# High and low parts of a weight unit stored in pairs in one tile, instead of in two tiles

## The reference

```python
# first block, per layer (D_MODEL 1024, D_FF 2816)
h = _rmsnorm(x, g_pre_ffn[l])
gate, up = jnp.split(h @ w_ffn_in[l], 2, axis=-1)
f = (jax.nn.silu(gate) * up) @ w_ffn_out[l]
x = x + _rmsnorm(f, g_post_ffn[l])
# second block, per layer
x = x + 0.5 * swiglu(rms_norm(x, ffn1_norm[l]), ffn1_w1[l], ffn1_w2[l])
x = x + hybrid_mixer(rms_norm(x, mix_norm[l]), ...)
x = x + 0.5 * swiglu(rms_norm(x, ffn2_norm[l]), ffn2_w1[l], ffn2_w2[l])
```

## Time and profile before

| what | value |
|---|---|
| two timed runs | 3475.27 and 3480.95 us, median 3478.11 us |
| the profiled execution | 3470.74 us, its span 3468.9 us |
| granted TensorE clock, mean | 0.994 |
| TensorE busy (matmuls) | 3365.4 us, 97% of the span |
| weight loads busy | 2884.7 us, 83% |
| VectorE busy | 2462.7 us, 71% |
| ScalarE busy | 1617.0 us, 47% |
| GpSimd busy | 55.9 us, 2% |
| moved by DMA | 318.95 MB, mean 92 GB/s |

### The profile page before, as it was taken

How to read it: one execution, slowest core, us unless ns; L and a number is a source line. 1 busy time by engine, 2 the same in 40 slices (tenths; PEclk the granted TensorE clock), 3 DMA queues, 4 the chain that set the end, 5 groups by cost and what they waited for, 6 DMA issues and landing times.

```text
span 3468.9 us, 49474 instructions
## 1 busy us (share of the span) xinstructions
PE 3365.4 (97%) x19557; PEld 2884.7 (83%) x19557; DVE 2462.7 (71%) x3512; ACT 1617.0 (47%) x2387; POOL 55.9 (2%) x84
## 2 busy tenths in 40 slices
PE   7999999999999999999999999999999989999999
PEld 5678988767998799887687899889988767788997
DVE  8669854759882888557895698559864888658863
ACT  4645543455562466326524356425542562335642
POOL 1000000000000000000000000000000000000000
PEclk9999999999999999999999999999999999999999
DMA  4123323212332233232133233323333213322332
GB/s 141 50 73 98 99 97 109 82 49 82 102 114 99 76 113 110 95 104 60 49 91 91 97 98 110 100 94 98 110 104 97 75 44 90 92 97 86 110 104 85
DMA packets 339642, 318.95 MB, mean 92 GB/s; under 512 B 31768, under 2 KB 312164, under 8 KB 339428
## 3 DMA queue, kind: packets, MB, share of 16 engines
q1 hardware_dynamic: 335588, 307.95, 28.0%
q0 software_dynamic: 2048, 6.16, 0.5%
q10 hardware_dynamic: 1792, 1.88, 0.2%
HBM read 313.84 MB, written 2.10 MB: 91 GB/s over the span
## 4 chain that ended last, share of the span: by engine, by line
PE 80%; DVE 15%; ACT 3%; issue 2%; DMA 0%; POOL 0%; DVEq 0%; POOLq 0%
PE products L797 31%; PE products L938 24%; PE products L836 7%; PE small L836 6%; PE small L938 4%; PE products L1199 2%; DVE w_lo L2152 2%; DVE seven_x L2404 1%; PE products L1396 1%; DVE conv L2939 1%; DVE X L2172 1%; DVE x_sums L2393 1%; ACT w_hi L1522 1%; PE small L1273 1%; DVE mla_prob L2599 1%
## 5 line engine op out<-in xcount | busy, mean ns | idle before, releaser
L2152 DVE TENSOR_TENSOR w_lo<-raw,w_hi 128x2048 fp32r<-128x2048 f32 x190 | 435.1, 2290 | 482.7 <-ACT w_hi L1522 482.4
L1522 ACT ACTIVATE w_hi<-raw 128x2048 fp32r<-128x2048 f32 x190 | 363.8, 1915 | 833.1 <-PE products L797 579.8
L797 PE MATMUL products<-a_hi,w_hi 128*128 128x512 f32 (+1 forms) x1216 | 490.8, 404 | 12.8 <-DVE a_lo L2212 10.1
L797 PE MATMUL products<-a_hi,w_lo 128*128 128x512 f32 (+1 forms) x1216 | 477.0, 392 | 0.0
L797 PE MATMUL products<-a_lo,w_hi 128*128 128x512 f32 (+1 forms) x1216 | 476.4, 392 | 0.0
L938 PE MATMUL products<-seven_x,w_hi 128*128 128x256 f32 x2592 | 465.6, 280 | 8.3 <-DVE w_lo L2433 3.2
L938 PEld LDWEIGHTS products<-seven_x,w_hi 128*128 128x128 f32 x2592 | 395.0, 188 | 12.2 <-DVE w_lo L2433 4.4
L938 PE MATMUL products<-seven_x,more_hi 128*128 128x256 f32 x1632 | 375.9, 279 | 3.6 <-ACT rs_b L1631 3.6
L938 PE MATMUL products<-seven_x,w_lo 128*128 128x256 f32 x1296 | 361.6, 279 | 0.0
L797 PEld LDWEIGHTS products<-a_hi,w_hi 128*128 128x128 f32 (+1 forms) x1216 | 229.9, 189 | 70.0 <-issue 16.7
L938 PEld LDWEIGHTS products<-seven_x,more_hi 128*128 128x128 f32 x1632 | 277.7, 188 | 4.8 <-ACT rs_b L1631 4.8
(11 more groups left out here) (463 smaller groups left out, 7228.8 us busy)
## 6 DMA issues: line engine op xcount, KB each, us to landing
raw<-in_ffn_w SPq DMA_DIRECT2D x244, 512.0 KB, 4.1
raw<-in_w_in SPq DMA_DIRECT2D x108, 512.0 KB, 4.6
raw<-in_w_ffn_in SPq DMA_DIRECT2D x88, 512.0 KB, 4.2
raw<-in_w_ffn_out SPq DMA_DIRECT2D x40, 512.0 KB, 4.5
raw<-in_w_out SPq DMA_DIRECT2D x32, 512.0 KB, 4.2
raw<-in_ffn_w SPq DMA_DIRECT2D x24, 384.0 KB, 3.5
raw<-in_w_mem_kv SPq DMA_DIRECT2D x8, 512.0 KB, 4.1
raw<-in_lru_w_out SPq DMA_DIRECT2D x8, 512.0 KB, 3.4
```

What stands on the lines that cost most here:

```text
L797: mm = pe.matmul(G[pair][0:m, into + b, 0:n], w[:, s, at:at + m], x, start=(first or into > 0) and k == 0 and q == 0, stop=(last or ends) ...
L1522: act.activation(w_hi[:, s, :], raw[:, s, :], ACT.Copy).then_inc(hi_ready, 1)
L2152: dve.tensor_tensor(w_lo[:, s, :], raw[:, s, :], w_hi[:, s, :].bitcast(F32), ALU.subtract).then_inc(lo_ready, 1)
```

## The change

The two tiles become one, `w_pairs`, of [128, 2 slots, 2048, 2]: the high part of a weight and its low part stand beside each other. `w_hi` and `w_lo` are views of it with 8 bytes from one element to the next, where there were 4. `w_sums` is the same view as `w_lo`, without the reduced format. The size is the same, 32 KB, and all tiles behind keep their places. The two scratch tiles of latent attention lie over slot 1 of the pairs. Nothing else is edited: instructions, their order on each engine, waits and loads from memory are the same, and the loads still go to `raw`, which keeps its form.

```diff
-    W_HI = top[0]
-    w_hi = place("w_hi", [P, 2, UNIT], F32R)
-    W_LO = top[0]
-    w_lo = place("w_lo", [P, 2, UNIT], F32R)
-    w_sums = place("w_sums", [P, 2, UNIT], at=W_LO)
+    W_PAIRS = top[0]
+    w_pairs = place("w_pairs", [P, 2, UNIT, 2], F32R)
+    w_hi, w_lo = w_pairs[:, :, :, 0], w_pairs[:, :, :, 1]
+    w_pair_sums = place("w_pair_sums", [P, 2, UNIT, 2], at=W_PAIRS)
+    w_sums = w_pair_sums[:, :, :, 1]
     ROWS_4 = 10 * P
     mla_prob = [place(f"mla_prob{i}", [P, ROWS_4], at=at)
-                for i, at in enumerate((W_LO + 4 * UNIT, W_HI + 4 * UNIT, BROADCASTS, BROADCASTS + 4 * ROWS_4))]
+                for i, at in enumerate((W_PAIRS + 12 * UNIT, W_PAIRS + 8 * UNIT, BROADCASTS, BROADCASTS + 4 * ROWS_4))]
```

## The result

The changed kernel takes 3968.89 us (two runs, 3968.1 and 3969.69) against 3478.11: a ratio of 1.141, 95% interval 1.136 to 1.146. It is 491 us slower. The forecast was no change; the time is also 19 us above the range, whose upper end was the rival of moving weights at half rate.

The account below looks back on a forecast made before the run. TensorE was taken to bound the kernel, with matmuls under way in 97% of the span. All terms were 0 but +1 us for ScalarE, on 3470.74 us: 3472, or 3479 us for a median; range 3460 to 3950 us.

Parts of the forecast that it names:

- the rival of moving weights at half rate: L836 and the values of L1396: 2016 matmuls at 226.7 ns more, 457 us, giving 3935 us; chance 0.16 near that.
- TensorE streams weights: L836 and L1396, 2016 matmuls with moving weights read in 8-byte steps: 0, 56 or 457 us; taken as 0.
- ScalarE's row: Profiled ScalarE copies of 512 columns: 592 ns contiguous, 620 ns in 8-byte steps, 28 ns or 5% more.
- The rule on cachelines: Two hits on each 16-byte line give full bandwidth, so all six kinds of access would stay at full rate.
- Places and stationary weights: Weight loads of L797, L938, L1199 and part of L1396 taken at 0; reads meeting in memory bounded at 3% either way.
- The working of the weight load: A strided load passes 8 bytes in 0.87 ns, 9.2 bytes a ns, a rate TensorE already reads at; taken as 0.
- a slower load shows in `seven`: Only 4 to 5 ns of 116.7 are spare in `seven`, 115 of 226.7 elsewhere, so only `seven` would show it.
- places of slots: Scratch tiles of latent attention stay over slot 1, and slots are handed over by the same semaphores: 0.
- VectorE at 0: VectorE's reads and writes of the parts (L2152, L2413 to L2441) cost 0; from above twice the time.
- ScalarE's splits: High parts written at L1522, L1616, L1621: 28 to 112 ns more a split of 2048, mostly hidden; +1 us taken.

Follow-up runs that it names:

- the kernel with slots: Against the kernel before: both parts contiguous, one behind the other in each slot of the pairs' region, in place of a tile for each part; 3474.59 us, ratio 0.999.

## Why the prediction was wrong

**TensorE streams weights: the step that failed.** It was named as the term that the trace does not settle, bounded by 0, 56 and 457 us, and taken as 0 with ScalarE's row as the nearest. It measured 2016 x 224.4 ns = 452 us. ScalarE goes at about half the moving operand's rate, and the bytes passed over in a ns, 18.6, spoke for the other bound; the row that was nearest in rate, TensorE's own 9.3 bytes a ns, should have counted for more than one near only in having the same step. The count, the price and the place of the rival were right; its chance of 0.16 was low for a term that the text itself called unsettled. The row was also read as "without loss" for VectorE, where it shows 5%. Its stated mechanism, memory delivered in stretches, holds with 16 bytes as the stretch in bf16 (226, 451 and 900 ns at steps 2, 4 and 8); for 4-byte operands it holds at step 2 and fails at steps 4 and 8, where 0.9 ns a column is all it ever costs.

**The rule on cachelines.** By the Trainium skill, SBUF — State Buffer, "Specifications (TRN2)", two hits on a line of 16 bytes suffice for full bandwidth. The runs agree within 5% for ScalarE (629 and 658 ns at steps 1 and 2, 1100 at step 4), for VectorE (691, 694, 1066) and for the weight load (188, 193, 310). They do not for the moving operand, with two hits 453 ns against 227; in bf16 it needed four, 226 ns, and took 451 with two. The measurement decides.

**Places and stationary weights: mis-sized.** The working of the weight load held: the walk of 9.2 bytes a ns was within what TensorE reads, the loads grew by 6 to 8 ns and not by 112. But that a slower load shows in `seven` "and nowhere else" was wrong. It took the two reads as independent. They are not: a load of step 2 slows a stream of 512 columns beside it from 226.7 to 233.3 ns, though the load, at 195 ns, is shorter than the matmul that hides it. The loss of 3% that the text allowed from places was put down for the memory's layout, with a price up or down, and was left out of the sum and of the rivals; it came as 43 + 19 us. These 62 us, less 14 of waits, 5 by which the moving weights cost less than the rival's 457 and 8 by which the medians differ less than the spans, put the time about 34 us above the rival's 3935, and so past the range's end.

**VectorE, ScalarE, places of slots.** VectorE at 0, right. ScalarE's splits grew by 102 to 157 ns where 28 to 112 were allowed, almost all of it hidden; alone, 512 columns gained 29 ns, so neither of the two ways of scaling gives 157 for 2048. The order of slots cost nothing, measured alone at 0.999. The scratch tiles were not tried by themselves; the kernel with slots had them in their new places too.

## What to carry to other kernels

Keep the operand that streams through TensorE so that each 16 bytes that it touches are used whole (in bf16 a half was enough, 226 ns against 217; three floats of four were not tried); a second operand beside it belongs in the next 16 bytes, not in the next 4. A step of 8 bytes is nearly free for ScalarE, VectorE and the weight load itself (5% at most with each alone), but such a load took 6.6 ns from each stream of 512 columns beside it. So before a layout is interleaved, count first the matmuls in which it moves, then those beside which it is loaded. And where a cost is bounded by 0 and by twice the time, ask which engine's rate the row of comparison was measured at.

## What the runs showed that was not expected

- The step of a 4-byte moving operand costs twice and no more: 453, 450, 461 and 431 ns at steps of 2, 3, 4 and 8 floats. In bf16 it goes on to 900 ns at step 8, at the full and at the half level of the granted clock alike. What makes the difference was not tried.
- With step 1, where the two operands stand relative to each other modulo 256 bytes is worth up to 3% of a matmul of 512 columns (226.7 to 234.2 ns) and 5% of one of 256 (113.6 to 120 ns).
- Long stretches of like matmuls settle in one of two paces that can differ from one feed-forward part to the next in one execution: 9.52 or 9.89 us a turn with the activations at 192 bytes, and 9.80 or 9.89 with them at 32 bytes, where the kernels with slots (two parts of six) and with pairs for L836 alone (one of six) fell to 9.89. What chooses is open.
